# Dense stage: the experts are picked before the shared expert's product, the logits stand in the middle of gate and up, and the next root comes behind the score

## The reference, cut to what matters

```
h      = layer_norm(ALPHA * x + cat @ w_out)
scores = sigmoid(h @ router_w)                      # 64 experts
eidx   = top 6 of (scores + router_bias), after the best 4 of 8 groups are kept
gates  = scores[eidx] / sum * 2.5
shared = (silu(h @ ws_gate) * (h @ ws_up)) @ ws_down
y      = layer_norm(ALPHA * h + shared + routed experts)
```

## Time and profile before

| | |
|---|---|
| median of 3 runs | 2389.51 us (2389.41 to 2390.86) |
| profiled execution | 2387.95 us, its span 2385.6 |
| mean granted clock of TensorE | 0.965 of 2.4 GHz |
| TensorE busy | 2220.5 us, 93% of the span |
| VectorE busy | 1407.0 us, 59% |
| ScalarE busy | 1131.2 us, 47% |
| dense stage | from about 672 to 1097 us of the span |

### The profile page before, as it was taken

The page is one execution under the profiler, slowest core; times in us unless marked ns, Lnnn a source line. Parts: engine busy times, 40 slices in busy tenths (PEclk is TensorE's granted clock), DMA queues, the critical chain, the costliest instruction groups (busy, mean ns, idle before and its releaser), DMA issues. The chain is left out here.

```text
span 2385.6 us, 34429 instructions
## 1 busy us (share of the span) xinstructions
PE 2220.5 (93%) x10800; PEld 1797.4 (75%) x10800; DVE 1407.0 (59%) x2590; ACT 1131.2 (47%) x1866; POOL 644.7 (27%) x597
## 2 busy tenths in 40 slices
PE   7999999999859999984999999999999999999970
PEld 5777777777648888873888888888888888888860
DVE  5343443443457778764666666666666666666637
ACT  4343333433333333322556655566555665556637
POOL 1111111111011233232333333333333333333320
PEclk9999999999979999996999999999999999999995
DMA  5011001000372233215899899998999999999858
GB/s 210 28 37 38 27 33 40 27 33 27 114 196 98 74 103 106 94 65 195 259 289 279 276 282 282 288 279 276 281 281 290 279 276 282 281 291 277 277 120 317
DMA packets 198913, 435.84 MB, mean 183 GB/s; under 512 B 39840, under 2 KB 44432, under 8 KB 197552
## 3 DMA queue, kind: packets, MB, share of 16 engines
q1 hardware_dynamic: 154992, 288.44, 36.0%
q0 software_dynamic: 43600, 145.95, 22.8%
q10 hardware_dynamic: 288, 1.05, 0.1%
HBM read 328.16 MB, written 109.39 MB: 183 GB/s over the span
## 5 line engine op out<-in xcount | busy, mean ns | idle before, releaser
L1583 PE MATMUL ex_psU<-ex_guh,ex_xh 128*128 128x512 f32 x1024 | 411.3, 402 | 3.7 <-DVE ex_xl L1568 3.7
L1585 PE MATMUL ex_psU<-ex_guh,ex_xl 128*128 128x512 f32 x1024 | 401.4, 392 | 0.0
L1584 PE MATMUL ex_psU<-ex_gul,ex_xh 128*128 128x512 f32 x1024 | 400.9, 392 | 0.0
L1556 DVE TENSOR_TENSOR ex_gul<-ex_raw,ex_guh 128x1024 fp32r<-128x1024 f32 x256 | 299.2, 1221 | 38.1 <-ACT ex_guh L1506 38.1
L1432 POOL DMA_INDIRECT acc_d<-ex_y,ex_use x128 | 206.2, 1611 | 401.0 <-ACT ex_y L1495 340.9
L1506 ACT ACTIVATE ex_guh<-ex_raw 128x1024 fp32r<-128x1024 f32 x256 | 253.5, 1061 | 30.2 <-DMA ex_raw<-w_experts 30.2
L1583 PEld LDWEIGHTS ex_psU<-ex_guh,ex_xh 128*128 128x128 f32 x1024 | 193.2, 189 | 40.8 <-DVE ex_xl L1568 4.4
L1585 PEld LDWEIGHTS ex_psU<-ex_guh,ex_xl 128*128 128x128 f32 x1024 | 193.0, 188 | 40.9
L1584 PEld LDWEIGHTS ex_psU<-ex_gul,ex_xh 128*128 128x128 f32 x1024 | 193.6, 189 | 36.9
L1454 POOL DMA_INDIRECT ex_xg<-h_d,ex_ent x128 | 198.3, 1549 | 67.2 <-issue 38.1
L1583 PE MATMUL ex_psY<-ex_dnh,ex_hdh 128*128 128x512 f32 x512 | 210.4, 411 | 1.7 <-DVE ex_hdl L1539 1.7
(11 more groups left out here) (309 smaller groups left out, 4211.4 us busy)
## 6 DMA issues: line engine op xcount, KB each, us to landing
ex_raw<-w_experts SPq DMA_DIRECT2D x192, 1024.0 KB, 11.7
acc_d<-de_acc SPq DMA_DIRECT2D x19, 512.0 KB, 3.0
mi_xr<-xT SPq DMA_DIRECT2D x17, 512.0 KB, 3.4
de_cr<-cat SPq DMA_DIRECT2D x17, 512.0 KB
de_xr<-x_rows SPq DMA_DIRECT2D x17, 512.0 KB, 4.2
h_d<-de_h POOLq DMA_DIRECT2D x17, 512.0 KB, 6.0
ln_t<-acc_d SPq DMA_DIRECT2D x17, 512.0 KB, 5.6
y<-ln_t SPq DMA_DIRECT2D x17, 512.0 KB, 4.2
```

Source lines behind the costliest of these rows:

```text
L1556: V.tensor_tensor(lo, src, hi.bitcast(F32), ALU.subtract).then_inc(s_split, 1)
L1583: nc.tensor.matmul(out, lh, rh, start=start, stop=False)
L1584: nc.tensor.matmul(out, lh, rl, start=False, stop=False)
L1585: return nc.tensor.matmul(out, ll, rh, start=False, stop=stop)
```

## The change

Three things are moved; nothing is added or left out. On TensorE the two products that make the logits move from behind the eight groups of `gu` to in front of the fourth. On ScalarE the square root for the next tile moves from in front of the score to behind it. On VectorE `pick(i)` moves from behind the two products that make `hid` to in front of them.

```diff
@@ scalar, step
                 nc.scalar.activation(lt[:], psR[:, 128:384], ACT.Copy).then_inc(S["router_copied"], 1)
-                if front:
-                    deviation(i + 1)
                 act.wait_ge(S["logit"], i + 1)
                 act.wait_ge(S["gscale"], i)
                 nc.scalar.activation(sc[:], psR[:, 0:NE], ACT.Sigmoid).then_inc(S["score"], 1)
+                if front:
+                    deviation(i + 1)
                 act.wait_ge(S["gu"], i + 1)
@@ vector, step
                     place(i - 1)
+                pick(i)
                 dve.wait_ge(S["sig"], i + 1)
                 V.tensor_tensor(hid[:], psU[:, 0:FF], sg[:], ALU.mult)
                 dve.drain()
                 V.tensor_tensor(hid[:], hid[:], psU[:, FF:2 * FF], ALU.mult).then_inc(S["hid"], 1)
-                pick(i)
@@ tensor, step
                 for kc in range(KC):
+                    if kc == 3:
+                        pe.wait_ge(S["router_copied"], i + 1)
+                        for part in range(2):
+                            last = nc.tensor.matmul(psR[:, 0:NE], lt[:, part * P:(part + 1) * P], eye2[:], start=(part == 0), stop=(part == 1))
+                        last.then_inc(S["logit"], 1)
                     last = three(psU[:], hT[:, kc, 0, :], hT[:, kc, 1, :], guh[:, kc, :], gul[:, kc, :], kc == 0, kc == KC - 1)
                 last.then_inc(S["gu"], 1)
-                pe.wait_ge(S["router_copied"], i + 1)
-                for part in range(2):
-                    last = nc.tensor.matmul(psR[:, 0:NE], lt[:, part * P:(part + 1) * P], eye2[:], start=(part == 0), stop=(part == 1))
-                last.then_inc(S["logit"], 1)
```

## The result

| | before | after |
|---|---|---|
| median | 2389.46 us of 4 runs (2388.64 to 2390.86) | 2455.68 us of 4 runs (2454.82 to 2463.38) |
| ratio | | 1.0284, 95% interval 1.0263 to 1.0305 |
| span of the profiled execution | 2385.6 us | 2453.6 us |
| mean granted clock | 0.965 | 0.959 |

The change costs 2.8%: 68.0 us of span. The page's first part of after: TensorE is busy for 18 us more than in the earlier trace rows, with the same number of instructions, and VectorE for as long as before.

The account below looks back on a forecast made before the run. TensorE, gapless at 21.87 us a tile, bounds the dense stage. 52.1 + 1.0 + 4.4 - 3.4 + 26 = +80 us on the profiled 2387.95 gives 2468, plus 1.6 to the median: 2470 us, range 2450 to 2485.

Parts of the forecast that it names:

- the low clock: TensorE behind each wait for hid: transposes and first matmuls run at 1.2 GHz, 1.9 us a tile, 26 us over 14.
- the ring: TensorE and VectorE waiting on each other from hidden_T to hidden_T: 25.59 us instead of 21.87, 52.1 us over fourteen periods.
- the first tile: First hidden_T of the loop comes later, at 730.94 instead of 729.97: 1.0 us.
- the end of the stage: Last tile: hdl no longer queues behind pick, rank and down start earlier, GpSimd's last scatter passes it on: -3.4 us.
- The signs named: Expected in the trace: hidden_T periods near 27.5 us, waits of 3.5 to 4, clock 0.50, ten transposes in some 2.4.
- The sixteenth: Sixteenth hidden_T, where TensorE already waits for hid: the whole of pick is added, 4.4 us.
- The logits and the root: Logits inside gu on TensorE, square root behind the score on ScalarE: price 0, std 1.2 us ahead of VectorE's question.
- The ring at the full clock: Rival: the ring's waits arise in the dense stage but the clock never falls, nothing of the 26 us; 2444 us; 8%.
- The clock doesn't come back: Rival: TensorE stays at the low clock nearly all of each tile, 41 us a tile; about 2660 us; 4%.
- No wait arises: Rival: hid still comes in time, TensorE stays gapless, only the last tile's gain is left; 2386 us; 3%.
- the reading by occupancy: Skill page's view, pointing to no wait: beside a gapless TensorE, a mere exchange on VectorE at 78% would be free.
- A shorter ring: Rival: VectorE saves something unseen behind pick, only a third of the loss stays; around 2415 us; 3%.

Follow-up runs that it names:

- The kernels with the scatter held: GpSimd's scatter held until the next project part 1 is done: kernel of before, 2386.0 and 2387.08 us; with logits and root moved and last-tile split, 2387.7 us.
- The filler: Changed kernel plus 13 matmuls with unused result in front of hidden_T, in TensorE's wait, in tiles 1 to 15: 2436.92 us, ratio 1.0166.
- the changed kernel's second profile: The changed kernel run once more, unchanged, beside its own kernel before on that chip: 2457.64 us, ratio 1.0302.
- the picking alone: Kernel of before with only pick moved in front of hid; logits and root stay as before: 2457.11 us, ratio 1.0252.
- the picking back: Changed kernel with pick behind hid again; logits and root stay moved: 2397.2 us, ratio 0.9999.
- the short dose: Changed kernel with hid made behind the first nine instructions of pick: 2397.48 us, ratio 1.0003.
- the two with the last tile alone: Changed kernel with pick first only in the last tile: wholly, 2396.78 us, ratio 0.9997; or with hid made inside that pick, 2396.25 us, ratio 0.9999.
- The half dose: Changed kernel with hid made in the middle of pick, behind the group penalties: 2403.64 us, ratio 1.0029.

## Why the prediction was right, and where its sizes were off

Forecast 2470 us (2450 to 2485) and slower; measured 2455.68. The mechanism was the right one, in the right place: no slack of more than 0.93 us, a ring of two engines, a low clock behind its wait. The forecast was 14 us too high. The sum was +80 us for the 68.0 measured between the spans: the low clock was put 9.9 us too high, the ring 4.3 and the first tile 1.0, while the end of the stage and the rest of the program, which the sum leaves out, came out 3.1 above it. Another 1.6 us were added because the profiled execution of before was that much under the median, while that of after, 2455.6, is at it. The step that was mis-sized most is the low clock, taken at 1.9 us in every one of 14 tiles.

**The ring** was to be 25.59 us and is 25.25 at the full clock. Its parts are as predicted but for `pick`. I took the mean of 4.60 us from where it stood before; in its new place it takes 4.23 in nearly every tile of the loop, less than either of the two lengths of the earlier trace rows. Its instruction at L1107 takes 172 ns each time, where it took 294 in the mean over 17 tiles before:

```profile
L1107 DVE TENSOR_SCALAR de_pen<-de_gr 128x8 f32<-128x8 f32 x15 | 2.6, 172 | 1.2
```

L1123 (263 instead of 307) and L1116 (195 instead of 247) go the same way. The kernels with the scatter held show one part of the reason. With `pick` in its old place and the scatter away from it the three instructions take 172, 255 and 196 ns, and `pick` 0.14 us less. The rows point to single instructions of the scatter: L1107 takes 0.31 us where it lies inside a DMA instruction of GpSimd, and 0.17 where it falls into the gap between two, though the scatter runs beside `pick` in both kernels. (L1123 doesn't follow this in every tile.)

```profile
926.98 0.97 POOL L971 DMA_INDIRECT table<-de_pay,de_dest  x1 [0.30 <-issue]
927.61 0.31 DVE L1107 TENSOR_SCALAR de_pen<-de_gr 128x8 f32<-128x8 f32 x1
```
```profile
962.86 0.99 POOL L971 DMA_INDIRECT table<-de_pay,de_dest  x1 [1.57 <-DVEq L1146]
963.96 0.17 DVE L1107 TENSOR_SCALAR de_pen<-de_gr 128x8 f32<-128x8 f32 x1
964.16 0.97 POOL L971 DMA_INDIRECT table<-de_pay,de_dest  x1 [0.30 <-issue]
```

The other 0.23 us are half of the 0.47 that `pick` took more in every second tile. It stays with the scatter held, and is idle time in part: 0.19 in front of L1121. In the new place neither is there; why is not known. So a duration read in one place is a bound for the other, not its value. In the sum: 14 x (25.25 - 21.87) = 47.3, and 0.5 more in the first two periods, instead of 52.1.

**The low clock** was to cost 1.9 us in each of 14 tiles, 26 us. Both factors were too big. A low stretch costs 26.86 - 25.25 = 1.6 us, and ten of the fourteen tiles have one: 16.1 us. The 1.9 held 1.4 for ten transposes, and that came of comparing unlike things: 2.40 us is the time from the start of the first to the end of the last, 1.01 only the time to the start of what follows. By the first measure they take 905.15 + 1.04 - 904.93 = 1.26 at the full clock, and the difference is 1.1.

```profile
905.15 1.04 PE L1295 MATMUL de_psT<-de_ident,de_h 128*128 128x128 f32 x8
```

Nor does the low clock fall on them alone: in the tile shown above `project` part 1 starts 1.30 us behind `hidden_T` (1.07 in the tile at 888.36, at the full clock), and the rest of the 1.6 is lost in its matmuls. The length of a stretch was read rightly (3.4 us); that each tile brings one was an assumption, carried over from the waits that the earlier trace rows shows. The filler shows that the term is the clock's: without waits the low stretches are gone, and all periods behind the first two are 25.2. The range held the time because its lower end allowed for a low clock "in some tiles only"; that this would happen in four of fourteen was not foreseen. The signs named were near, and two of them off: waits of 3.2 us for the 3.5 to 4, and ten transposes in 2.4 us only in the tile that begins at 780.97 (1.64 in the one shown).

**The first tile** was to cost 1.0 and cost 0.0. The stage happened to be 0.8 us ahead there: its second `residual` starts at 717.51 before and at 716.67 after. Relative to that, the cost is 0.8. **The sixteenth** `hidden_T` cost 4.6, for 4.4.

**The end of the stage** was to gain 3.4 us and gained 1.7. `rank` did come 3.1 us earlier. In this profile the step that failed is "which GpSimd's last scatter passes on": the last scatter starts 11.24 us behind the last `hidden_T` before (1085.72) and 8.84 after (1151.70), so 2.4 of the 3.1 arrive there, and 1.7 at the next stage. Behind the earlier `rank` VectorE had to wait 0.63 us for the scatter of the tile before, which it used to meet finished:

```profile
1147.91 0.17 DVE L1141 SCALAR_TENSOR_TENSOR de_dest<-de_d,de_drop 128x6 int32<-128x6 f32 x1 [0.63 <-DMA table<-de_pay,de_dest]
```

In the changed kernel's second profile this wait is missing: the last scatter starts 8.13 us behind the last `hidden_T`, so all 3.1 arrive there, and the next stage starts 19.98 us behind it, 2.9 earlier than the 22.9 of before. So 1.7 is what one profile shows, not the size of the effect.

**The logits and the root** were priced at nothing, and with the picking undone they cost nothing. On ScalarE, the counterpart of the earlier trace rows:

```profile
955.24 0.22 ACT L1034 ACTIVATE de_sc<-de_psR 128x64 f32<-128x64 f32 x1 [2.07 <-PE de_psR L1316]
955.49 1.28 ACT L1001 ACT_TABLE_LOAD   x1
956.78 0.20 ACT L1001 ACTIVATE de_rs<-de_rs 128x1 f32<-128x1 f32 x1
957.00 1.28 ACT L1039 ACT_TABLE_LOAD   x1
```

std is there at 956.98 and VectorE asks for it at 958.15: the predicted 1.2 us are left. The load of 1.28 us ends at 956.77, and the root starts at 956.78.
A drain of some 1380 ns, which the Trainium skill (ScalarE: Activation LUTs, What ACT_TABLE_LOAD costs) has besides the load, shows neither behind it nor in front of it (the root ends at 956.98, the next load starts at 957.00): the trace disagrees with it, and the 3 us that it would have added didn't come.

**The rivals.** The ring at the full clock (2444) is refuted by the windows, though it describes four of the fourteen periods. "The clock doesn't come back" is refuted: it is at 1.00 for the 19.10 us behind the low stretch. "No wait arises" is refuted by the fourteen waits.
With it falls the reading by occupancy (the Trainium skill, Perfetto Trace Analysis, Identifying Performance Opportunities): VectorE, at 78% beside a gapless TensorE, set the period as soon as its result was late. "A shorter ring" was right in its sign, 0.34 us a tile, and far from its size.

## What to carry to other kernels

Ahead of reordering two pieces on an engine that isn't the bound, read how long before its use the result that will come later is ready today. What is moved past it beyond this slack (here 4.23 - 0.93 = 3.3 us, and the period grew by 3.4) is paid in full, once per tile, if the consumer stands in front of the work that this engine waits for next; average idle time doesn't count. Waits of 3.2 us on TensorE can bring a low clock on top, here a third as much again as the waits themselves, and it is worth splitting a loss into idle time and longer busy time before explaining it. And a difference between two durations is only good if both are taken from the same point to the same point.

## What the runs showed of the hardware that was not expected

**Low stretches skip tiles in a pattern.** Behind six waits of 3.2 us the share of the clock in the first 3.4 us is 1.00, 0.56, 0.62, 0.69, 1.00, 0.57 (windows above): the low stretch begins a little later in each tile, 0.4, 0.9 and 1.3 us behind `hidden_T` in the three tiles between the two without, and after the third or fourth one there is a tile without. The changed kernel in its second run and the picking alone show the same order of long and short periods. Waits of 0.82 to 0.86 us in thirteen tiles, and one of 1.17, never lowered the clock. Why every fourth or fifth wait is spared stays open.

**A release that comes 1.5 us late on some chips.** Where the unchanged kernel takes 2397 us its periods are 22.5 us instead of 21.87, which is 14 x 0.6 = 8 us. (Of the two chips of that kind it was profiled on one; on the other the kernel with the picking back has the same periods.) It arises in one place. In the unchanged kernel run again there, the last matmul into psC starts at 914.92 and ends at 915.31; ScalarE's `t`, which waits for it, starts at 916.94, 1.6 us later, and the trace names no local releaser:

```profile
914.92 0.39 PE L1242 MATMUL de_psC<-de_woh,de_cl 128*128 128x512 f32 x1
```
```profile
916.94 1.12 ACT L997 ACTIVATE de_t<-de_psA,de_ra 128x1024 f32<-128x1024 f32 x1 [6.05 <-remote]
```

In the kernel before of the earlier trace rows the same pair is 0.13 us apart (911.68 and 911.81), though GpSimd issues its last indirect DMA 1.5 us ahead there too:

```profile
911.29 0.39 PE L1242 MATMUL de_psC<-de_woh,de_cl 128*128 128x512 f32 x1
```
```profile
911.81 1.12 ACT L997 ACTIVATE de_t<-de_psA,de_ra 128x1024 f32<-128x1024 f32 x1 [4.56 <-PE de_psC L1242]
```

The delay of 1.5 us is longer than the slack of 0.93, and the 0.6 that is left is the longer period. On these chips the delay shows only in kernels in which GpSimd issues its last indirect DMA of the tile within 1.5 us ahead of that matmul's end (the unchanged one, the picking back, the short dose, the two with the last tile alone). The half dose, where it is issued 2.5 us ahead, and the filler and the picking alone, where it is 4.9 us or more, have 0.13 between the matmul's end and `t`. In the short dose the two are 0.84 us apart, a delay of 0.7. So the picking alone takes 2457 us where the unchanged kernel takes 2397, and the changed kernel takes 2456 and 2458 where it takes 2389 and 2386: the ratios 1.025, 1.028 and 1.030 differ mostly by what the unchanged kernel does. That the scatter's transfers cause it is a guess from this coincidence: the three runs with the scatter held met chips on which the unchanged kernel isn't slow, so the theory was not tested. A ratio of two kernels can thus be smaller on one chip than on another because the kernel it is taken to has a loss of its own there.
